# Routing inside the mix stage's block, ranks by products with ones, the last tile by halves, dummy products, the first slab in parts

## The chip, the cores and the metric

The kernel runs on one core of one Trainium2 chip. The metric is the device time of one launch in microseconds, here the median of three runs. The profiler adds one traced execution, from which the busy times and waits below come.

## The reference, cut to what matters

The program is two layers of a network on 512 tokens of width 1024, all in float32. The change lies in the first: behind its token mixer comes a feed-forward layer in which each of 16 experts chooses its 64 tokens.

```python
# y_lat: output of the token mixer before its norm (the mix stage computes it and all up to h)
x_lat = x_lat + gt1 * rmsnorm(y_lat, norm_post_mix)
h = rmsnorm(x_lat, norm_pre_ffn) * (1.0 + sc2) + sh2

def expert_choice_ffn(h, w_router, w_gate, w_up, w_down):
    cap = 2 * 512 // 16                                   # 64 tokens for each expert
    aff = softmax(h @ w_router, axis=-1)                  # [512, 16]
    top_aff, top_idx = lax.top_k(aff.T, cap)              # each expert's 64 best tokens
    xin = h[top_idx]                                      # [16, 64, 1024]
    g, u = xin @ w_gate, xin @ w_up                       # 16 experts, [1024, 1024] each
    y = ((silu(g) * u) @ w_down) * top_aff[..., None]
    return zeros(512, 1024).at[top_idx].add(y)
```

Order within an expert's 64 rows is free, since the rows are added back by index.

## The kernel before

The program is a sequence of stages, each in a block of its own; at a block's end all engines wait for each other. Inside a block every engine has a list of instructions written out by hand, and semaphores order them. The stages that matter here are `mix_and_project`, `route` and `experts`.

**`mix_and_project`** turns the mixer's rows (`turn_mix`, four tiles of 128 tokens), multiplies them by `w_out` (`product_hi`, `product_lo`, signalled half by half through `n.ready`), and takes each tile t through `norm_steps`: squares and root on ScalarE (`act_first`), gating and the addition to `x` on VectorE (`dve_gate`, `dve_add`, signalled by `n.added`), then the second norm's root (`act_root`) and eight transposes of `x` on TensorE (`turn`). ScalarE copies the first four turned blocks into `h2T` and VectorE the others (both called `take`). `logits(t)` multiplies them by the router's weights, `take_parts` copies the partial sums, `folded(t)` adds the four groups in a product and `take_logits` writes the tile's row of logits. The second norm's rows are also split into three bf16 parts (`act_full`, `dve_full`, `act_top`, `less`, `act_mid`, `low`), which the gather reads.

**`route`** makes the softmax over the 16 experts (VectorE, with one Exp on ScalarE), turns the affinities so that experts lie on 16 partitions, copies them to `left`, and finds each expert's 64 best tokens in eight rounds of a maximum of eight and a replacement by -1. `chosen` is then 1 where a value was replaced; a running sum over the tokens (`tensor_tensor_scan`) times `chosen` is the token's place, 1 to 64. Four transposes bring the places back to tokens on partitions (`posT`). While VectorE does this, TensorE runs 14 dummy products (`keep_busy`, a product of the identity into a bank that nobody reads). SyncE loads the first expert slab in five parts (`m.opening`: three of 512 KB, two of 256 KB) at the start of this stage.

**`experts`** streams 96 slabs of 2 MB (w_gate, w_up, w_down, two halves each, for 16 experts). Experts go in pairs. `mark(i)` on VectorE makes the one-hot matrix of a pair from `posT`. `gather(i)` on TensorE takes the pair's rows out of the three parts: 96 products into banks 0 and 1, then 4 with the identity (the transposed one-hot, `spread`) and 12 for the affinities. `take_in` copies the results: ScalarE blocks 0 to 3 of `xin`, then `spread` and the slot affinities; VectorE blocks 4 to 7. Then follow `up_product` for w_gate and w_up, the hidden rows' transposes and `down_product`. A slab has one of ten places. Slabs 0 to 9 are issued before the stage (0 in the opening places; 5, 4, 1, 2, 3 and 8 in the mix stage, 6, 7 and 9 in `route`). From slab 10 on, SyncE issues a slab when the one that held its place has been used: slab 10 waits for the second half of the first up product.

The order of the loads on SyncE's queue in `mix_and_project` before:

```python
sp.wait_ge(gated_out, TT);        stream(sp, m, I, S_EXP + 5, S_EXP + 6)
sp.wait_ge(n.ready, 2 * TT - 1);  stream(sp, m, I, S_EXP + 4, S_EXP + 5); stream(sp, m, I, S_EXP + 1, S_EXP + 2)
sp.wait_ge(n.ready, 2 * TT);      stream(sp, m, I, S_EXP + 2, S_EXP + 4)
stream(sp, m, I, S_EXP + 8, S_EXP + 9)
```

Of the kernel before, what the change touches and what calls it, by code (L numbers as in the profile page):

```python
# [1344 lines left out]
def norm_steps(m, tag, x, xn, st, gate=None, gated=None, weight=None, quarters=False):  # L1345
# [31 lines left out]
    def act_root(act, t):  # L1377
        act.wait_ge(n.added, t + 1)
# [23 lines left out]
    def dve_add(dve, t):  # L1402
# [7 lines left out]
        dve.wait_ge(n.gated, 2 * t + 2)  # L1410
        dve.scalar_tensor_tensor(out=x[:, t, :], in0=gated(t), scalar=st[:, 4, t:t + 1], in1=x[:, t, :],
# [13 lines left out]
    def turn(pe, t):  # L1425
# [115 lines left out]
def mix_and_project(nc, m, I):  # L1541
# [41 lines left out]
    lg = m.logits = m.rows_after[0][:, :].rearrange("p (t e) -> p t e", e=EXPERTS)  # L1583

# [12 lines left out]
    with nc.Block() as block:  # L1597
        @block.sync
        def _(sp):
# [4 lines left out]
            for r in range(2):  # L1604
                sp.dma_start(m.w_router[:, 4 * r:4 * r + 4, 0:EXPERTS],
                             I["w_router"][0].rearrange("(r p j) e -> r p j e", r=2, j=4)[r]).then_inc(m.router_in, 16)
            sp.wait_ge(gated_out, TT)
            stream(sp, m, I, S_EXP + 5, S_EXP + 6)
            sp.wait_ge(n.ready, 2 * TT - 1)
# [3 lines left out]
            stream(sp, m, I, S_EXP + 2, S_EXP + 4)  # L1613
            stream(sp, m, I, S_EXP + 8, S_EXP + 9)

        @block.gpsimd
        def _(pool):
            pool.memset(m.w_router[:, :, :], 0.0).then_inc(zeroed, 1)

        @block.tensor  # L1620
        def _(pe):
# [80 lines left out]
            for t in range(1, TT):  # L1702
# [11 lines left out]
                logits(t - 1)  # L1714
            folded(TT - 2)
            n.turn(pe, TT - 1)
            logits(TT - 1)
            folded(TT - 1)

        @block.scalar  # L1720
        def _(act):
# [51 lines left out]
            for t in range(TT):  # L1773
# [7 lines left out]
                if t:  # L1781
                    take_parts(t - 1)
                n.act_root(act, t)
# [3 lines left out]
            take(TT - 1)  # L1787
            take_parts(TT - 1)
            m.parts.act_full(act, TT - 1)

        @block.vector
        def _(dve):
# [100 lines left out]
            take_logits(TT - 1)  # L1893


def route(nc, m, I):
# [10 lines left out]
    chosen, place = [m.small(name, [E, T], at) for name, at in (("chosen", 0), ("place", 2 * KB))]  # L1907
    ones = m.ones[0:E, 0:1].to_broadcast([E, T])
    top = m.rows_after[2][0:E, 32:40]

    expd = m.sem("logit_exp_ready")
# [6 lines left out]
    place_ready = m.sem("place_ready")  # L1918
    place_turned = m.sem("place_turned")
    logit_less = m.sem("logit_less_max")  # L1920
    with nc.Block() as block:
        @block.sync
        def _(sp):
            first = slab_source(I, S_EXP)
            for k in range(3):
# [1942 lines left out]
```

## Time and profile before

| what | us |
| --- | --- |
| median of three runs (lowest, highest) | 1714.55 (1711.69, 1719.66) |
| profiled execution, its own time | 1718.3 |
| profiled execution, span of the trace | 1716.4 |
| TensorE busy (matmul) | 1622.8 |
| VectorE busy | 875.1 |
| ScalarE busy | 640.5 |
| GpSimd busy | 81.6 |
| granted TensorE clock, mean | 0.978 of full |

Times inside the trace count from the span's start. A busy TensorE is not TensorE at its peak: its matmuls overlap, and at the lower of its two clocks (1.2 and not 2.4 GHz, shown as 0.5) it is busy twice as long. A wait shows as the idle time of an engine, with the instruction that ended it. A transfer has an issue on SyncE's queue (`SPq`) and a time to landing, counted from the issue's start.

### The profile page before, as it was taken

How to read it: one execution, taken by the hardware profiler on the slowest of the kernel's cores; microseconds unless marked ns; L12 is line 12 of the kernel's file. 1: busy time of each engine (PE TensorE's matmuls, PEld its weight loads, DVE VectorE, ACT ScalarE, POOL GpSimd, SP SyncE). 2: the span in 40 equal slices, each digit the busy share in tenths (PEclk: the TensorE clock that was granted, in tenths of full speed). 3: DMA queues.
4: the chain of work that ended last, by engine and by line, in shares of the span. 5: the costliest groups of instructions: out<-in, count | busy, mean ns of one | idle time of the engine just before them, and what ended most of it. 6: DMA issues, size and time to landing. Idle time of an engine off the chain costs nothing. (4 is left out here: it accounts for less than half of the span.)

```text
span 1716.4 us, 26072 instructions
## 1 busy us (share of the span) xinstructions
PE 1622.8 (95%) x11074; PEld 1156.3 (67%) x11074; DVE 875.1 (51%) x1287; ACT 640.5 (37%) x1085; POOL 81.6 (5%) x69
## 2 busy tenths in 40 slices
PE   6999999988988999999999989998989999999997
PEld 4787888767764444334433378887878798888886
DVE  4445454189752122221221477754537638585768
ACT  4325774322551111011101244324465435454545
POOL 0010000000010000000000012211130000000000
PEclk9999999989989999999999989999999999999999
DMA  9221011246268999999999932210001270505111
GB/s 371 97 98 50 1 50 50 98 188 227 94 263 370 429 430 429 432 429 430 429 430 430 411 135 98 99 50 1 3 4 50 62 258 1 196 2 195 41 58 50
DMA packets 68764, 323.38 MB, mean 188 GB/s; under 512 B 6604, under 2 KB 11036, under 8 KB 55080
## 3 DMA queue, kind: packets, MB, share of 16 engines
q1 hardware_dynamic: 67768, 319.51, 46.7%
q8 instruction: 88, 1.44, 0.3%
q10 hardware_dynamic: 880, 2.20, 0.3%
q14 instruction: 28, 0.23, 0.0%
HBM read 315.41 MB, written 6.29 MB: 187 GB/s over the span
## 5 line engine op out<-in xcount | busy, mean ns | idle before, releaser
L3623 DVE TENSOR_TENSOR mlp_w_lo<-ring,mlp_w_hi 128x1024 fp32r<-128x1024 f32 x84 | 102.3, 1221 | 93.6 <-ACT mlp_w_hi L3558 93.4
L2190 PE MATMUL bank<-ring,xinT 128*64 128x512 f32 x528 | 117.8, 594 | 3.5 <-DMA ring<-w_gate 3.5
L2190 PE MATMUL bank<-expert_slab,xinT 128*64 128x512 f32 x480 | 107.2, 594 | 1.7 <-DMA expert_slab<-w_gate 1.7
L259 PE MATMUL bank<-h4T_hi,mlp_w_hi 128*128 128x512 f32 (+1 forms) x288 | 105.5, 366 | 0.3 <-PEq L3208 0.3
L259 PE MATMUL bank<-h4T_lo,mlp_w_hi 128*128 128x512 f32 (+1 forms) x288 | 105.2, 365 | 0.0
L259 PE MATMUL bank<-h4T_hi,mlp_w_lo 128*128 128x512 f32 (+1 forms) x288 | 105.2, 365 | 0.0
L3558 ACT ACTIVATE mlp_w_hi<-ring 128x1024 fp32r<-128x1024 f32 x84 | 88.8, 1057 | 38.6 <-PE bank L3512 38.6
L259 PE MATMUL bank<-hT_hi,in_w_hi 128*128 128x512 f32 (+1 forms) x256 | 96.9, 379 | 1.8 <-ACT v L630 1.8
L259 PE MATMUL bank<-hT_hi,in_w_lo 128*128 128x512 f32 (+1 forms) x256 | 90.0, 352 | 0.0
L259 PE MATMUL bank<-hT_lo,in_w_hi 128*128 128x512 f32 (+1 forms) x256 | 89.7, 350 | 0.0
L2190 PEld LDWEIGHTS bank<-ring,xinT 128*64 128x64 f32 x528 | 37.8, 137 | 75.6 <-issue 71.7
L3512 PE MATMUL bank<-mlp_w_hi,mlp_rows_hi 128*128 128x512 f32 x224 | 87.4, 390 | 1.4 <-DVE x L3679 1.4
L603 DVE TENSOR_TENSOR in_w_lo<-ring,in_w_hi 128x1024 fp32r<-128x1024 f32 x31 | 42.4, 1368 | 87.9 <-ACT in_w_hi L597 87.9
L3512 PE MATMUL bank<-mlp_w_hi,mlp_rows_lo 128*128 128x512 f32 x224 | 87.2, 389 | 0.0
L3512 PE MATMUL bank<-mlp_w_lo,mlp_rows_hi 128*128 128x512 f32 x224 | 87.1, 389 | 0.0
L2190 PEld LDWEIGHTS bank<-expert_slab,xinT 128*64 128x64 f32 x480 | 34.4, 137 | 67.3 <-issue 65.2
L2292 ACT ACTIVATE expert_out_hi<-bank 64x512 fp32r<-64x512 f32 x32 | 18.9, 591 | 146.8 <-PE bank L2210 146.3
L2351 DVE TENSOR_TENSOR expert_out_lo<-bank,expert_out_hi 64x512 fp32r<-64x512 f32 x32 | 22.0, 689 | 100.3 <-ACT expert_out_hi L2292 99.8
L2338 DVE SCALAR_TENSOR_TENSOR expert_hidden<-bank,slot_affinity,gate_sig 128x512 f32<-128x512 f32 x16 | 18.0, 1124 | 99.9 <-PE bank L2190 56.4
L2210 PE MATMUL bank<-expert_slab,expert_hiddenT 128*64 128x512 f32 x288 | 66.1, 607 | 2.4 <-DMA expert_slab<-w_down 2.4
L597 ACT ACTIVATE in_w_hi<-ring 128x1024 fp32r<-128x1024 f32 x31 | 32.7, 1056 | 90.0 <-PE bank L259 87.7
L259 PE MATMUL bank<-h3T_hi,gdn_w_hi 128*128 128x512 f32 x160 | 62.4, 390 | 0.0
(520 smaller groups left out, 3633.3 us busy)
## 6 DMA issues: line engine op xcount, KB each, us to landing
expert_slab<-w_down SPq DMA_DIRECT2D x18, 2048.0 KB, 28.1
ring<-w_up SPq DMA_DIRECT2D x17, 2048.0 KB, 22.6
ring<-w_gate SPq DMA_DIRECT2D x16, 2048.0 KB, 21.3
expert_slab<-w_gate SPq DMA_DIRECT2D x15, 2048.0 KB, 22.8
expert_slab<-w_up SPq DMA_DIRECT2D x15, 2048.0 KB, 24.2
ring<-mlp_w SPq DMA_DIRECT2D x15, 2048.0 KB, 8.5
ring<-w_down SPq DMA_DIRECT2D x14, 2048.0 KB, 25.3
ring<-w_ada SPq DMA_DIRECT2D x8, 2048.0 KB, 7.8
```

The source lines that it names most:

```text
L259: mm = pe.matmul(out, x, y, start=(start and i == 0), stop=(stop and i == 2))
L597: act.activation(shaped_buffer(q)[0], slab_part(m, s, i, by_rows), ACT.Copy).then_inc(m.in_w_hi_ready, 1)
L603: dve.tensor_tensor(lo, slab_part(m, s, i, by_rows), hi, ALU.subtract).then_inc(m.in_w_lo_ready, 1)
L2190: mm = pe.matmul(bank[half * H:(half + 1) * H, b, :], xin[:, 4 * r + k, (e % 2) * H:(e % 2 + 1) * H], expert_part(m, s, k, half), start=(r ...
L2210: mm = pe.matmul(bank[half * H:(half + 1) * H, 7, :], hidT[:, k, r * H:(r + 1) * H], expert_part(m, s, k, half), start=(r == 0 and k == 0) ...
L2292: act.activation(m.y[0][r * H:(r + 1) * H, half * COLS:(half + 1) * COLS], bank[half * H:(half + 1) * H, 7, :], ACT.Copy).then_inc(y_hi, 1)
L2338: dve.scalar_tensor_tensor(out=hid[:, :].rearrange("p (j q) -> p q j", j=4), in0=bank[:, b + 1, :].rearrange("p (q j) -> p q j", j=4), sca ...
L2351: dve.tensor_tensor(m.y[1][dst], bank[half * H:(half + 1) * H, 7, :], m.y[0][dst], ALU.subtract).then_inc(y_lo, 1)
L3512: mm = pe.matmul(bank[:, 4 + 2 * pair + t, :], a[:, k, tok], b[:, k, :], start=(anew and i % 2 == 0 and k == 0 and n == 0), stop=(i % 2 == ...
L3558: act.activation(buffer_of(unit)[0], weight_source(unit), ACT.Copy).then_inc(w_hi, 1)
L3623: dve.tensor_tensor(lo, weight_source(unit), hi, ALU.subtract).then_inc(w_lo, 1)
```

## The change

- **Last tile by halves.** In tile 3 `dve_add` adds `x` in two instructions of 512 columns; `turn` starts its first four transposes behind the first, ScalarE's `take(3)` comes ahead of `act_root(3)`.
- **Routing in the mix stage's block.** `route` has no block of its own. It gives each engine a list that is appended to that of `mix_and_project`; VectorE's begins with a wait for the last logits. ScalarE begins with an Exp on a value that nobody reads; `act_full(3)` comes behind the real Exp.
- **Ranks by products.** The first maximum and replacement read the turned affinities from their bank, with no copy. What is left after the rounds is turned back to tokens on partitions and compared with 0 there (`chosen`, [128, 64]). One product with `m.upto` (ones where row <= column) and three with ones, accumulated, give the running sum over tokens; one multiplication gives `posT`.
- **Dummy products.** `keep_busy` takes a number of columns. There is one of 512 and two of 256 columns in the tail of the mix stage, two of 512 ahead of the affinities' transposes, 13 (before 14) behind them, and one of 256 ahead of the first gather.
- **First slab in parts.** Parts 0, 1 and 3 are issued behind the last `turn_mix`, part 2 behind the third tile's `low`, part 4 behind the last logits and `act_full(3)`; slab 8 now comes after part 4.
- **Gather.** In every `gather` the 4 and 12 short products come first. `gathered` is signalled twice, for blocks 0 to 3 and 4 to 7; ScalarE copies `spread` and the affinities first. The wait for VectorE's blocks (`xin_v`) moves to the second slab of the w_gate product.

```diff
-def keep_busy(pe, m, b, n):
+def keep_busy(pe, m, b, n, cols=COLS):
...
-        pe.matmul(m.bank[:, b, :], m.ident, m.table[:, 0:COLS], start=True, stop=True)
+        pe.matmul(m.bank[:, b, 0:cols], m.ident, m.table[:, 0:cols], start=True, stop=True)
...
     def act_root(act, t):
-        act.wait_ge(n.added, t + 1)
+        act.wait_ge(n.added, t + 2 if quarters and t == TT - 1 else t + 1)
...
+        if quarters and t == TT - 1:
+            for i in range(2):
+                dve.scalar_tensor_tensor(out=x[:, t, cols(i)], in0=gated(t)[:, cols(i)], scalar=st[:, 4, t:t + 1], in1=x[:, t, cols(i)],
+                                         op0=ALU.mult, op1=ALU.add).then_inc(n.added, 1)
+            return
...
         for k in range(KD):
+            if quarters and t == TT - 1 and k == 4:
+                pe.wait_ge(n.added, TT + 1)
...
             sp.wait_ge(gated_out, TT)
             stream(sp, m, I, S_EXP + 5, S_EXP + 6)
+            sp.wait_ge(mix_turned, 2 * TT)
+            for i in (0, 1, 3):
+                opening(i)
             sp.wait_ge(n.ready, 2 * TT - 1)
             stream(sp, m, I, S_EXP + 4, S_EXP + 5)
             stream(sp, m, I, S_EXP + 1, S_EXP + 2)
             sp.wait_ge(n.ready, 2 * TT)
             stream(sp, m, I, S_EXP + 2, S_EXP + 4)
+            sp.wait_ge(m.parts.low_done, TT - 1)
+            opening(2)
+            sp.wait_ge(logits_out, TT)
+            sp.wait_ge(m.parts.full, 2 * TT)
+            opening(4)
             stream(sp, m, I, S_EXP + 8, S_EXP + 9)
+            stream(sp, m, I, S_EXP + 6, S_EXP + 7)
+            sp.wait_ge(m.x_kept, 16 * TT)
+            stream(sp, m, I, S_EXP + 7, S_EXP + 8)
+            stream(sp, m, I, S_EXP + 9, S_EXP + 10)
...
+            keep_busy(pe, m, 5, 1)
             folded(TT - 2)
+            keep_busy(pe, m, 5, 1, COLS // 2)
             n.turn(pe, TT - 1)
+            keep_busy(pe, m, 5, 1, COLS // 2)
             logits(TT - 1)
             folded(TT - 1)
+            choice.tensor(pe)
...
+                if t == TT - 1:
+                    take(t)
                 n.act_root(act, t)
...
-            take(TT - 1)
             take_parts(TT - 1)
-            m.parts.act_full(act, TT - 1)
+            choice.scalar(act)
...
+    def tensor(pe):
+        keep_busy(pe, m, 5, 2)
+        pe.wait_ge(aff_ready, 1)
+        for t in range(TT):
+            mm = pe.transpose(bank[0:E, 1, t * P:(t + 1) * P], aff[:, t, :], m.ident)
+        mm.then_inc(aff_turned, 1)
+        keep_busy(pe, m, 5, CAP // 8 + 5)
+        pe.wait_ge(ranked, 1)
+        for t in range(TT):
+            mm = pe.transpose(bank[:, 2, t * E:(t + 1) * E], left[:, t * P:(t + 1) * P], m.ident[0:E, 0:E])
+        mm.then_inc(ranked_turned, 1)
+        pe.wait_ge(chosen_ready, 1)
+        pe.matmul(bank[:, 3, 0:TT * E], m.upto, chosen, start=True, stop=False)
+        for t in range(1, TT):
+            mm = pe.matmul(bank[:, 3, t * E:TT * E], m.ones[:, :], chosen[:, 0:(TT - t) * E], start=False, stop=(t == TT - 1))
+        mm.then_inc(place_ready, 1)
+
+    def scalar(act):
+        act.activation(unused, m.eps[:, :], ACT.Exp)
+        act.wait_ge(logit_less, 1)
+        act.activation(ex[:, :, :], lg[:, :, :], ACT.Exp).then_inc(expd, 1)
+        parts.act_full(act, TT - 1)
...
-            link(dve.tensor_copy(left[:, :], bank[0:E, 1, :]))
-
-            for _ in range(CAP // 8):
-                link(dve.max(top[:, :], left[:, :]))
-                link(dve.match_replace(left[:, :], top[:, :], left[:, :], -1.0))
-            link(dve.tensor_scalar(chosen[:, :], left[:, :], 0.0, None, ALU.is_lt))
-
-            link(dve.tensor_tensor_scan(place[:, :], ones, chosen[:, :], 0.0, ALU.mult, ALU.add))
-            dve.tensor_tensor(place[:, :], place[:, :], chosen[:, :], ALU.mult).then_inc(place_ready, 1)
-            dve.wait_ge(place_turned, 1)
-            dve.tensor_copy(m.posT[:, :, :], bank[:, 2, 0:TT * E].rearrange("p (t e) -> p t e", e=E))
...
+        for i in range(rounds):
+            now = left[:, :] if i else bank[0:E, 1, :]
+            link(dve.max(top[:, :], now))
+            taken = dve.match_replace(left[:, :], top[:, :], now, -1.0)
+            if i + 1 < rounds:
+                link(taken)
+        taken.then_inc(ranked, 1)
+        dve.wait_ge(ranked_turned, 1)
+        dve.tensor_scalar(chosen, bank[:, 2, 0:TT * E], 0.0, None, ALU.is_lt).then_inc(chosen_ready, 1)
+        dve.wait_ge(chosen_ready, 1)
+        dve.wait_ge(place_ready, 1)
+        dve.tensor_tensor(m.posT[:, :, :], bank[:, 3, 0:TT * E].rearrange("p (t e) -> p t e", e=E),
+                          chosen.rearrange("p (t e) -> p t e", e=E), ALU.mult)
...
+                    if k % 4 == 3:
+                        mm.then_inc(gathered, 1)
...
+                    if r and e % 2 == 0 and name == "g":
+                        pe.wait_ge(xin_v, e // 2 + 1)
...
+            keep_busy(pe, m, 5, 1, COLS // 2)
             gather(0)
```

## Rows read from the trace of the kernel before

**Rows 1.** The page, forty slices of the span (tenths of the transfer engines' time)

```profile
DMA  9221011246268999999999932210001270505111
```

**Rows 2.** Windows: us, busy time of each engine, granted clock, DMA share, GB/s

```profile
475.00:489.00 14.00, 14.00 (x86) 11.47 (x85) 8.35 (x14) 8.16 (x15) 0.00 (x0) 1.00 0.10 39
...
538.00:542.00 4.00, 4.00 (x20) 1.55 (x18) 0.00 (x0) 0.12 (x1) 0.00 (x0) 1.00 0.05 20
...
546.00:760.00 214.00, 211.95 (x1308) 90.13 (x1306) 48.36 (x75) 27.83 (x66) 0.00 (x0) 1.00 1.01 430
760.00:965.00 205.00, 193.88 (x1114) 79.61 (x1108) 49.23 (x76) 26.17 (x59) 0.00 (x0) 0.99 1.01 429
```

**Rows 3.** Waits in 760 to 972 us: total, times, longest

```profile
PE bank L2190 <- DMA ring<-w_gate: 3.5, 3, 1.3
```

**Rows 4.** Timeline of SyncE's queue: start and length of issue, us

```profile
510.82 0.82 SPq L229 DMA_DIRECT2D expert_slab<-w_down  x1
...
541.88 3.76 SPq L229 DMA_DIRECT2D ring<-w_gate  x2
```

**Rows 5.** Transfers issued in 511 to 512 and 541 to 542.5 us: to landing

```profile
expert_slab<-w_down SPq DMA_DIRECT2D x1, 2048.0 KB, 27.7
...
ring<-w_gate SPq DMA_DIRECT2D x1, 2048.0 KB, 8.1
```

**Rows 6.** Timeline of the last tile's end, all engines: start, length in us

```profile
497.37 1.28 DVE L1411 SCALAR_TENSOR_TENSOR x<-out_gated,out_stats,x 128x1024 f32<-128x1024 f32 x1
...
498.69 1.06 ACT L1379 ACTIVATE xn<-x 128x1024 f32<-128x1024 f32 x1 [1.53 <-DVE x L1411]
...
498.71 1.61 PE L1435 MATMUL bank<-table,x 128*128 128x128 f32 x8 [1.11 <-DVE x L1411]
...
501.20 1.08 PE L1661 MATMUL bank<-h2T,w_router 128*32 128x128 f32 x16 [0.88 <-DVE h2T L1806]
...
503.31 0.23 DVE L1824 SCALAR_TENSOR_TENSOR router_rows<-bank,out_stats,router_bias 128x16 f32<-128x16 f32 x1 [1.38 <-PE bank L1673]
```

**Rows 7.** Timeline of earlier tiles, TensorE

```profile
476.02 1.19 PE L1435 MATMUL bank<-table,x 128*128 128x128 f32 x8
...
482.65 0.64 PE L1661 MATMUL bank<-h2T,w_router 128*32 128x128 f32 x16
```

**Rows 8.** Timeline of the routing stage, all engines

```profile
503.94 1.28 ACT L1949 ACT_TABLE_LOAD   x1 [0.27 <-PEq L1597]
503.97 0.22 DVE L1970 TENSOR_REDUCE router_rows<-router_rows 128x4 f32<-128x64 f32 x1 [0.43 <-PEq L1597]
...
505.23 0.26 ACT L1949 ACTIVATE router_rows<-router_rows 128x64 f32<-128x64 f32 x1
...
506.26 1.02 PE L1938 MATMUL bank<-table,affinity 128*16 128x128 f32 x4 [2.99 <-DVE affinity L1975]
...
507.08 13.42 PE L266 MATMUL bank<-table 128*128 128x512 f32 x28
507.33 0.68 DVE L1977 COPY aff_left<-bank 16x512 f32<-16x512 f32 x1 [1.12 <-PE bank L1938]
...
508.04 0.68 DVE L1980 MAX8 router_rows<-aff_left 16x8 f32<-16x512 f32 x1
...
519.98 0.42 DVE L1982 TENSOR_SCALAR chosen<-aff_left 16x512 f32<-16x512 f32 x1
...
522.86 0.22 DVE L1987 COPY placeT<-bank 128x64 f32<-128x64 f32 x1 [0.51 <-PE bank L1943]
```

**Rows 9.** Timeline of the first gather and the next one

```profile
524.13 0.61 PE L2172 MATMUL bank<-onehot,xn_top 128*128 128x128 bf16 x4 [1.31 <-DVE onehot L2301]
...
534.76 3.65 PE L2190 MATMUL bank<-opening,xinT 128*64 128x512 f32 x16 [1.78 <-ACT spread L2266]
...
563.12 0.40 PE L2172 MATMUL bank<-onehot,xn_top 128*128 128x128 bf16 x4
...
569.09 3.65 PE L2210 MATMUL bank<-ring,expert_hiddenT 128*64 128x512 f32 x16
```

More of the change, by code:

```diff
@@ L1906, in route @@
     left = m.arena("aff_left", [E, T], 90)
-    chosen, place = [m.small(name, [E, T], at) for name, at in (("chosen", 0), ("place", 2 * KB))]
-    ones = m.ones[0:E, 0:1].to_broadcast([E, T])
+    chosen = m.rows_after[0][:, :]
     top = m.rows_after[2][0:E, 32:40]
+    r = Shared()
     expd = m.sem("logit_exp_ready")
@@ new lines, in scalar @@
+    def scalar(act):
[3 more added lines that the diff above has]
+        parts.act_full(act, TT - 1)
+        parts.act_top(act, TT - 1)
+        act.activation(m.ident_narrow[:, :], m.ident, ACT.Copy)
+        act.wait_ge(aff_ready, 1)
+        act.activation(m.aff_parts[:, 0], aff[:, :, :], ACT.Copy).then_inc(aff_top, 1)
+        parts.act_mid(act, TT - 1)
+        act.wait_ge(aff_less, 1)
+        act.activation(m.aff_parts[:, 1], less[:, :, :], ACT.Copy).then_inc(aff_mid, 1)
@@ L1990, in output_norms @@
+    r.tensor, r.scalar, r.gpsimd, r.vector = tensor, scalar, gpsimd, vector
+    return r
 def output_norms(m, done):
@@ L2168, in gather @@
                     pe.wait_ge(summed, NS * (i - 1))
-                for k in range(KD):
-                    for part in range(3):
-                        for t in range(TT):
-                            mm = pe.matmul(bank[:, k // 4, (k % 4) * P:(k % 4 + 1) * P], xn2_part(m, part, t, k), m.onehot[:, t, :],
-                                           start=(part == 0 and t == 0), stop=(part == 2 and t == TT - 1))
-                mm.then_inc(gathered, 1)
                 for t in range(TT):
@@ L2181, in gather @@
                                        start=(part == 0 and t == 0), stop=(part == 2 and t == TT - 1))
-                mm.then_inc(onehot_used, 1)
+                mm.then_inc(spread_turned, 1)
+                for k in range(KD):
+                    for part in range(3):
+                        for t in range(TT):
+                            mm = pe.matmul(bank[:, k // 4, (k % 4) * P:(k % 4 + 1) * P], xn2_part(m, part, t, k), m.onehot[:, t, :],
+                                           start=(part == 0 and t == 0), stop=(part == 2 and t == TT - 1))
+                    if k % 4 == 3:
+                        mm.then_inc(gathered, 1)
             def up_product(e, name, b, part_ready, ready):
@@ L2257, in take_in @@
             def take_in(i):
-                act.wait_ge(gathered, i + 1)
-                for k in range(4):
-                    ins = act.activation(xin[:, k, :], bank[:, 0, k * P:(k + 1) * P], ACT.Identity,
-                                         scale=m.a2[:, k:k + 1], bias=m.mod[:, 16 + k, 0:1])
-                ins.then_inc(xin_a, 1)
-                act.wait_ge(onehot_used, i + 1)
+                act.wait_ge(spread_turned, i + 1)
                 if i >= 2:
@@ L2270, in take_in @@
                                        bank[r * H:(r + 1) * H, 3, r:r + 1], ACT.Copy).then_inc(slot_aff_ready, 1)
+                act.wait_ge(gathered, 2 * i + 1)
+                for k in range(4):
+                    ins = act.activation(xin[:, k, :], bank[:, 0, k * P:(k + 1) * P], ACT.Identity,
+                                         scale=m.a2[:, k:k + 1], bias=m.mod[:, 16 + k, 0:1])
+                ins.then_inc(xin_a, 1)
             take_in(0)
```

93 lines of the change are left out of this document (33 added, 60 removed).

## The prediction, made before the changed kernel was timed

> **What bounds the kernel now.** I read the page first, then windows over the stretch that the change touches, then who waits, then the transfers one by one, then the timeline. In the page's forty slices the DMA row is full from the fourteenth slice to the twenty-third [rows 1]: that is the expert stage, which streams 96 slabs of 2 MB. The windows sharpen it [rows 2]: from 546 to 965 us the transfer engines are at 1.01 and move 429 to 430 GB/s. TensorE is idle for 2.05 of 214 us up to 760, and for 11.1 of 205 us after it; among the longest waits of that second part is one for slabs [rows 3], and up to 760 the same view has no wait for a slab at all. So TensorE starts with ten slabs in memory, catches up with the transfers at 760, and from there runs at their pace: the end of the stage is the arrival of the last slab. Everything behind it hangs on that, so a microsecond of the stage's end is one of the span.
>
> When does the last slab land? The transfers run without a hole except one: in 538 to 542 the share is 0.05 [rows 2]. All slots are full there, and the queue waits for TensorE to release the first. The tenth slab of the preload was issued at 510.82 and took 27.7 us, so it landed at 538.5; the next was issued at 541.88 and took 8.1, landing at 549.98 [rows 4, 5]. At 429 GB/s a slab (2.097 MB) takes 4.89 us. The hole thus costs 549.98 - 538.5 - 4.89 = 6.6 us. After it the queue is never empty, so the rest of the stage is a rigid train behind that one issue.
>
> That gives the account. Gain = how much earlier that slab lands, and two things limit it: **A**, how much earlier TensorE gets there (the slot is released two slabs into its first up product); **B**, what the transfers can do: 6.6 us of hole, plus what is moved ahead of the full stretch. In 475 to 489 us the share is 0.10 [rows 2], so parts 0, 1 and 3 of the first slab (512 + 512 + 256 KB = 1.31 MB), now issued behind the last turn of the mix rows, at about 476, are free there and take 1.31/0.429 = 3.1 us from the full stretch. B = 9.7 us.
>
> **The change part by part, for A.**
>
> *Last tile by halves.* Before, x is added in one instruction at 497.37 to 498.65, the eight transposes take 1.61 us, the logits start at 501.20 and the last row of logits is out at 503.54 [rows 6]. After: the first 512 columns are ready at about 498.06 (half of 1.28 and 0.05 of overhead), four transposes 0.6 (eight take 1.19 at the full clock [rows 7]) run while the second half is added (to 498.75); the other four end at 499.4 and not 500.3, and the logits, which wait for VectorE's copy of them, start at about 500.2: 1.0 earlier. At full clock they take 0.64 and not 1.08 [rows 6, 7]: 0.4 more. ScalarE now copies its half (an estimate from the square's 1.06 for twice the columns: 0.6) ahead of the square and the root, so these end 0.6 later, at about 500.85, just as the logits end: no loss, but no slack. Saved: 1.4 (bounds: 0.9 without the clock, 1.6).
>
> *Routing inside the block.* Between 503.54 and 505.23 lie the block's end (0.43), two VectorE steps of 0.22 and a table load of 1.28 that only starts at 503.94 [rows 8]. Now a throwaway Exp is put right behind ScalarE's copy of the logit parts (about 501.2), so the load is over at 502.5 and the throwaway at 502.75; the logits are at 502.1, the maximum taken off at 502.65. Exp starts at about 502.75 and not 505.23: saved 2.5 in all, 1.1 of it here. The row of Exp starts 0.01 after the load ends. The Trainium skill (ScalarE: Activation LUTs, What ACT_TABLE_LOAD costs) puts a drain of 1.38 behind each load; by it, as an estimate, Exp would start at 504.1, and the sum would be 8.4 and not 9.7.
>
> *Transposes of the affinities, and no copy.* Four transposes of 1.02 at the lower clock become about 0.6 if the clock holds: 0.4. VectorE's copy of 0.68 goes, since the first maximum reads the bank [rows 8]; I take a maximum from a bank at the copy's price from a bank, which is that of the maximum (0.68 both). With the gap, 0.7. Sum so far 3.6. The eight rounds (508.04 to 519.98, 11.9 us) stay.
>
> *Ranks by products.* From 519.98 to 523.08, 3.1 us: comparison, scan, product on 16 partitions, four transposes, copy [rows 8]. After: four transposes (at most 0.5, by the copy's wait), a comparison on 64 columns (0.22 like the copy), four products, one multiplication (0.22). No row has these products; 16 of 128 columns take 0.64 [rows 7], and four with 64 columns or fewer can hardly take less than 0.3; I take 0.6. With four hand-overs of 0.05: 1.7. Saved 1.4 (1.1 to 1.7). Sum 5.0.
>
> *Gather.* Its first matmul is at 524.13, and the up product starts at 534.76, 10.6 us later; the next pair's gather takes 569.09 - 563.12 = 5.97 [rows 9]. Of the difference 1.8 is the wait on ScalarE's `spread` (the row of 534.76), which the new order inside `gather` takes away: the one-hot products come first, so `spread` and the first four blocks of `xin` are copied under the rest, and VectorE's four blocks are only asked for by the second slab, 3.4 us later. The other 2.9 is the clock: the first 96 products ran mostly at 1.2 GHz (0.61 for four [rows 9], 0.39 later). If the new dummies (one of 256 columns ahead of the gather) and the shorter gaps hold the clock, both are saved: 4.7; if not, 1.8. Sum A = 9.7, or 6.8.
>
> *What costs nothing.* The other dummies: one ahead of each short piece of the tail, two ahead of the affinity transposes, 13 behind them. Fourteen took 13.42 [rows 8]; less 1.2 for a start of about 2.4 us at the lower clock, one takes 0.87 at full speed and 1.74 at half (estimates). Two from 501.65 end at 503.4, the affinities come at 503.7; 13 from 504.35 end at 515.65, the last round at 516.3. They are covered by 0.3 and 0.65 us, which is thin (see rivals). Later gathers: same work in another order, with a down product of 7 us behind each. SyncE: slab 8 is now queued behind part 4, which waits for the last logits and for `act_full` behind Exp (about 504.2, where before it was issued with slabs 2 and 3), and slabs 6, 7 and 9 after it. The transfers issued by then (four slabs from 489, part 2) last until about 511, so 6 us of cover; each microsecond beyond is one of loss. One barrier less for all engines is in the 2.5 above.
>
> **The sum.** A = 9.7 and B = 9.7 agree, so I forecast 9.6. Against its own execution: 1716.4 - 9.6 = 1706.8 span, with the 1.9 around it 1708.7. That execution is 3.75 above the median; on the median, 1714.55 - 9.6 = 1705.0.
>
> **Rivals.**
> 1. *The clock falls ahead of the gather.* TensorE has some 1.5 us of work in the 3.6 between the 13th dummy and the gather. It fell in the tail of before after short pieces and gaps (0.5 from 500 us by the doubled logits, rows 6). Then A = 6.8: 1714.55 - 6.8 = 1707.8.
> 2. *The dummies become the chain.* If the clock already falls in the tail, logits and fold cost 0.6 more, two dummies at 1.2 GHz take 2 x 1.74 = 3.5 and hold the affinity transposes until 505.8, these take 1.02, the first maximum is at 506.9 (saved 1.1, not 3.6), the 13 dummies end at 519.4 and the rounds at 518.8 (0.6 more lost). A = 1.1 - 0.6 + 1.4 + 1.8, with 2.9 if the clock is back: 3.7 to 6.6, so 1708 to 1711. The Trainium skill (TensorE: Matmul & The Clock Gate, Part 4: PE-mode transpose) says that transposes don't count as busy for the clock; by it the tail, half of which is transposes, points to this rival; in rows 6 the clock falls around transposes, but behind gaps too, so they don't decide it.
> 3. *Slower: the 13 dummies at 1.2 GHz.* At 1.74 each they are 22.6 us. For every microsecond that the clock stays low in them the ranks are 0.5 later; from 5.0 us saved (rival 2 with the low clock in the gather too: 519.98 - 506.9 - 11.3 = 1.8, and 1.4, and 1.8) the change is at zero after 10 us at the low clock, and at 22.6 it is 6.3 slower: 1720.9. Against it: before, some 2.4 us of the same dummies were low.
> 4. *The hole stays.* If slots are released no earlier in effect, or the queue behind part 4 runs dry as much as is won, only the 3.1 us of moved parts are left: 1711.5. Against it: the 6 us of cover.
> 5. *A drain behind the throwaway load*, as the skill's rule in the part on routing: 8.4, so 1706.2. Mechanism: ScalarE idle behind its load. The Exp row speaks against it.
>
> **Chances.** The forecast 0.52 (its own range 1704 to 1706.5), rival 1 0.22, rival 2 0.08, rival 3 0.04, rival 4 0.06, rival 5 0.03, and 0.05 for more than B (gaps elsewhere in the span that shift). A measurement tells 0.5% (8.6 us, so 1706.0) from no change. The forecast lies 1 us beyond that and the runs shown scatter by 2.9 below and 5.1 above their median, so 0.8 of its chance counts as faster: 0.42, with the last case 0.47 faster. Slower is rival 3 and 0.02 for scatter, 0.06; the rest, 0.47, is within. Range: from 1705.0 less the lower scatter, 1702, to the end of rivals 2 and 4, 1711.5.
>
> **What the changed profile would show.** Parts 0, 1, 3 issued near 476; no window under a share of 0.9 between 491 and 960; the first reuse of a slot issued near 532.2 and landing near 540.3; Exp with its load ended before; first up product near 525 with no wait; four gather products of 0.39 from the first on and the granted clock at 1.00 from 497 to 530. TensorE's waits for slabs after 750 as before. A clock of 0.5 around 502 or 520 is rival 2 or 1; a dummy ending right at the affinity transposes or the last transposes is rival 2 or 3. I am wrong if the last slab's landing moves by less than the first reuse does.

## The result, and the profile after

The changed kernel takes 1702.5 us (median of four runs, 1702.2 to 1706.3), the kernel before 1713.4 on the same chip (1711.7 to 1719.7). The ratio is 0.9938, with a 95% interval from 0.9919 to 0.9956, which is 7.5 to 13.9 us. The forecast was 1705.0.

The profiled execution has a span of 1700.4 us against 1716.4, but 6.6 of these 16.0 are no part of the change: slab 4 is issued at 482.50 and was at 489.09, and every instruction ahead of it that TensorE's path depends on is the same in both. What differs is the granted clock, the third number from the end in the windows up to that issue, before and after:

```profile
0.00:489.09 489.09, 455.86 (x3363) 364.88 (x3363) 267.66 (x412) 219.63 (x368) 15.26 (x20) 0.97 0.33 118
0.00:482.50 482.50, 450.89 (x3363) 360.99 (x3364) 267.24 (x412) 219.77 (x368) 15.59 (x20) 0.99 0.34 123
```

It goes with the execution and not with the kernel: a second trace of the changed kernel (x_again, below) has the issue at 482.9, and its variants have it at 483.3 to 488.2, the last of them at a clock of 0.97. So all distances in this part are counted **from the issue of slab 4**. By that count the end of the span comes at 1217.9 and was at 1227.3: 9.4 earlier.

The windows of the changed kernel, with the columns of [rows 2]:

```profile
475.00:489.00 14.00, 14.00 (x79) 11.07 (x78) 7.89 (x12) 7.08 (x13) 0.00 (x0) 1.00 0.49 187
489.00:534.00 45.00, 42.06 (x273) 22.59 (x274) 20.48 (x48) 13.28 (x30) 4.92 (x5) 0.96 0.99 412
534.00:546.00 12.00, 12.00 (x60) 4.11 (x58) 1.81 (x2) 1.18 (x2) 0.00 (x0) 1.00 1.00 429
546.00:760.00 214.00, 211.28 (x1298) 89.82 (x1296) 52.83 (x83) 28.95 (x67) 0.00 (x0) 1.00 1.01 430
760.00:965.00 205.00, 191.40 (x1100) 78.80 (x1100) 47.49 (x72) 30.63 (x65) 0.00 (x0) 0.99 1.01 428
```

The hole of 538 to 542 us, at 20 GB/s, is no longer there, but a dip is left in its place that these long windows hide. Around the issue of slab 10 (the first that reuses a slot) the transfers move 235 GB/s for 3 us and not 430:

```profile
527.50:530.50 3.00, 3.00 (x16) 1.00 (x14) 0.69 (x1) 0.60 (x1) 0.00 (x0) 1.00 0.76 235
```

In the last stretch TensorE still idles for 13.6 of 205 us, and it waits for slabs as in [rows 3]:

```profile
PE bank L2226 <- DMA ring<-w_gate: 3.6, 3, 1.3
...
PE bank L2226 <- DMA expert_slab<-w_gate: 2.4, 2, 1.3
```

So the stage's end is still the arrival of the last slab. SyncE's queue (start and length of issue), with below it the time to landing of the transfers issued in 527.5 to 528.3 us:

```profile
469.26 1.29 SPq L1619 DMA_DIRECT2D opening<-w_gate  x3
482.50 0.33 SPq L229 DMA_DIRECT2D expert_slab<-w_gate  x1
...
490.03 7.96 SPq L1619 DMA_DIRECT2D opening<-w_gate  x2
498.04 0.44 SPq L229 DMA_DIRECT2D ring<-w_down  x1
...
505.09 0.43 SPq L229 DMA_DIRECT2D expert_slab<-w_down  x1
...
527.83 0.33 SPq L229 DMA_DIRECT2D ring<-w_gate  x1
```

```profile
ring<-w_gate SPq DMA_DIRECT2D x1, 2048.0 KB, 8.1
```

Slab 10 is issued at 527.83, a distance of 45.33 where it was 52.79 [rows 4]: **7.46 us earlier**, and it takes the same 8.1 to land [rows 5]. The timeline between, with the columns of [rows 6]:

```profile
490.77 1.42 DVE L1413 SCALAR_TENSOR_TENSOR x<-out_gated,out_stats,x 128x512 f32<-128x512 f32 x2
...
493.87 0.65 PE L1688 MATMUL bank<-h2T,w_router 128*32 128x128 f32 x16 [0.44 <-DVE h2T L1838]
...
494.86 1.28 ACT L1974 ACT_TABLE_LOAD   x1
...
495.33 0.23 DVE L1856 SCALAR_TENSOR_TENSOR router_rows<-bank,out_stats,router_bias 128x16 f32<-128x16 f32 x1
...
496.16 0.20 ACT L1974 ACTIVATE router_rows<-eps 128x1 f32<-128x1 f32 x1
496.27 0.24 ACT L1976 ACTIVATE router_rows<-router_rows 128x64 f32<-128x64 f32 x1
...
497.29 0.60 PE L1960 MATMUL bank<-table,affinity 128*16 128x128 f32 x4 [0.18 <-DVE affinity L2002]
...
497.73 11.32 PE L266 MATMUL bank<-table 128*128 128x512 f32 x26
497.93 0.69 DVE L2007 MAX8 router_rows<-bank 16x8 f32<-16x512 f32 x1 [0.70 <-PE bank L1960]
...
509.18 0.66 DVE L2008 MATCH_REPLACE8 aff_left<-router_rows,aff_left 16x512 f32<-16x512 f32 x1
509.90 0.42 PE L1965 MATMUL bank<-table,aff_left 16*128 16x16 f32 x4 [0.85 <-DVE aff_left L2008]
510.36 0.23 DVE L2013 TENSOR_SCALAR router_rows<-bank 128x64 f32<-128x64 f32 x1 [0.51 <-PE bank L1965]
510.63 0.43 PE L1968 MATMUL bank<-router_rows,table 128*128 128x64 f32 x2 [0.32 <-DVE router_rows L2013]
510.91 0.79 PE L1970 MATMUL bank<-router_rows,ones 128*128 128x48 f32 x6
511.81 0.23 DVE L2016 TENSOR_TENSOR placeT<-bank,router_rows 128x64 f32<-128x64 f32 x1 [1.23 <-PE bank L1970]
...
513.09 0.40 PE L2203 MATMUL bank<-ident_narrow,onehot 128*128 128x128 bf16 x4
...
514.10 0.63 PE L2213 MATMUL bank<-onehot,xn_low 128*128 128x128 bf16 x4
...
520.70 3.65 PE L2226 MATMUL bank<-opening,xinT 128*64 128x512 f32 x16
```

Three things are to be seen. The table load is over before Exp is due, and the throwaway follows it in 0.02 us. The four products of the running sum (with `m.upto` and with ones, the rows of L1968 and L1970) take 1.07 us from 510.63, the longest piece of the ranks. And the gather starts with four products in 0.40 us, but from 514.10 four take 0.63: TensorE has fallen to the lower of its two levels (1.2 GHz, not 2.4) in the midst of products that follow each other without a gap. The granted clock of the windows shows both, the full clock in the tail and the fall:

```profile
489.00:497.50 8.50, 7.44 (x57) 4.03 (x57) 5.29 (x15) 5.98 (x13) 0.00 (x0) 1.00 1.01 425
497.50:510.00 12.50, 11.65 (x32) 5.05 (x29) 11.39 (x24) 2.78 (x7) 4.92 (x5) 1.00 1.00 419
510.00:521.00 11.00, 9.97 (x128) 9.20 (x130) 1.33 (x4) 3.93 (x10) 0.00 (x0) 0.84 1.01 432
```

### The profile page after: what moved, and what is told of

Same layout as the page of the kernel before. It is cut to its first block and busy times, and to the rows that moved or that the text cites. A ratio compares the mean times of both kernels' runs of the same rounds, so it can differ in the third digit from the quotient of the medians.

```text
span 1700.4 us, 26105 instructions
## 1 busy us (share of the span) xinstructions
PE 1616.7 (95%) x11092; PEld 1148.4 (68%) x11092; DVE 872.1 (51%) x1285; ACT 641.8 (38%) x1086; POOL 82.0 (5%) x69
## 3 DMA queue, kind: packets, MB, share of 16 engines
q1 hardware_dynamic: 67768, 319.51, 47.2%
## 5 line engine op out<-in xcount | busy, mean ns | idle before, releaser
L2374 DVE SCALAR_TENSOR_TENSOR expert_hidden<-bank,slot_affinity,gate_sig 128x512 f32<-128x512 f32 x16 | 18.0, 1124 | 99.9 <-PE bank L2226 56.4
L3619 ACT ACTIVATE mlp_relu<-bank 128x512 f32<-128x512 f32 x32 | 19.1, 598 | 115.8 <-PE bank L259 115.8
```

The costliest lines, as they stand in the source:

```text
L2374: dve.scalar_tensor_tensor(out=hid[:, :].rearrange("p (j q) -> p q j", j=4), in0=bank[:, b + 1, :].rearrange("p (q j) -> p q j", j=4), sca ...
L3619: act.activation(r[:, u % 2, :], bank[:, u % 4, :], ACT.Relu).then_inc(relu, 1)
```

## The experiments

Every kernel is told by the same chain: the gather starts, the first up product starts, slab 10 is issued, the slab before it lands, slab 10 lands, the last slab lands. In us from the issue of slab 4, worked out of each trace's rows; landings are issue plus time to landing. Each row is one trace. The ratio is to the kernel before, from four runs of the changed kernel and six to twelve of each other one; the kernel before had medians of 1713.4, 1714.5, 1714.4 and 1712.5 in the four sessions.

| kernel | gather | it lasts | up product | slab 10 issued | slab 9 lands | slab 10 lands | last lands | ratio |
| --- | --- | --- | --- | --- | --- | --- | --- | --- |
| before | 35.0 | 10.6 | 45.7 | 52.8 | 49.4 | 60.9 | 479.2 | 1 |
| x_parts_alone | 35.0 | 10.6 | 45.7 | 52.8 | 46.7 | 60.6 | 478.7 | 0.9993 |
| x_delay_first | 37.5 | 6.0 | 43.5 | 50.6 | 46.2 | 58.7 | 477.0 | 0.9992 |
| x_delay_second | 30.6 | 7.6 | 38.2 | 45.3 | 46.9 | 54.6 | 474.1 | 0.9966 |
| x_parts_late | 30.6 | 7.5 | 38.1 | 45.2 | 49.6 | 55.7 | 473.4 | 0.9972 |
| x_both_late | 30.6 | 6.8 | 37.4 | 44.5 | 50.2 | 56.4 | 473.1 | 0.9974 |
| x_delay_small | 30.6 | 6.0 | 36.6 | 43.7 | 46.2 | 53.8 | 472.1 | 0.9964 |
| x_scan | 31.5 | 7.4 | 39.0 | 46.1 | 46.7 | 54.2 | 471.7 | 0.9963 |
| x_no_dummies | 33.1 | 6.0 | 39.1 | 46.2 | 46.6 | 54.7 | 471.6 | 0.9966 |
| x_gather_old | 30.6 | 8.4 | 39.0 | 46.1 | 47.1 | 54.2 | 471.5 | 0.9958 |
| changed | 30.6 | 7.6 | 38.2 | 45.3 | 46.9 | 53.4 | 471.0 | 0.9938 |
| x_again | 30.6 | 7.6 | 38.2 | 45.3 | 47.2 | 53.8 | 470.8 | 0.9934 |
| x_delay_late | 30.6 | 7.5 | 38.1 | 45.2 | 46.6 | 53.8 | 470.4 | 0.9952 |
| x_warm | 30.8 | 6.0 | 36.8 | 43.9 | 46.4 | 52.5 | 469.7 | 0.9946 |

**x_again.** The changed kernel, unedited.

> The changed kernel once more. Theory (the stage's end follows the first reuse of a slot, which came 7.5 us earlier in the trace): 7.5 to 9.5 us under the kernel before, a ratio of 0.9945 to 0.9956. Rival (more is won than the expert stage shows, for the medians differ by 10.9): 10 us or more, 0.994 or less.

Measured: 1704.7 us, ratio 0.9934 (0.9915 to 0.9952). Its chain is that of the changed kernel to 0.4 us. The ratio is the rival's (11.3 us) and not the theory's; the interval reaches into the theory's band, but slab 10 lands only 7.1 earlier than before, and that is outside it.

**x_no_dummies.** The new dummies left out; the 13 behind the affinities' transposes stay.

```diff
-            keep_busy(pe, m, 5, 1)
             folded(TT - 2)
-            keep_busy(pe, m, 5, 1, COLS // 2)
             n.turn(pe, TT - 1)
-            keep_busy(pe, m, 5, 1, COLS // 2)
...
-        keep_busy(pe, m, 5, 2)
         pe.wait_ge(aff_ready, 1)
...
-            keep_busy(pe, m, 5, 1, COLS // 2)
             gather(0)
```

> The changed kernel without the new dummy products in the tail, ahead of the affinity transposes and ahead of the first gather; the 13 stay. Theory (they hold TensorE's clock through the tail): logits, fold and transposes at 1.2 GHz again, 1.2 us later, and the gather low to about 3 us instead of 1.6: the first reuse 1.5 to 3 us later and the span as much longer than the changed kernel's. Rival (the clock does not hang on them, and they only fill): the same within 0.5 us. Second rival (they sit in the chain): up to 1 us shorter.

Measured: 1709.5 us, ratio 0.9966 (0.9951 to 0.9980). The windows of its tail and of its rounds, and TensorE's timeline:

```profile
493.00:500.00 7.00, 3.88 (x31) 2.82 (x32) 3.63 (x11) 5.49 (x10) 0.00 (x0) 0.63 0.99 403
500.00:514.00 14.00, 14.00 (x31) 5.84 (x30) 11.39 (x24) 2.19 (x6) 4.92 (x5) 0.82 1.02 425
```

```profile
499.18 1.02 PE L1956 MATMUL bank<-table,affinity 128*16 128x128 f32 x4 [1.86 <-DVE affinity L1998]
499.99 13.86 PE L266 MATMUL bank<-table 128*128 128x512 f32 x26
513.79 0.42 PE L1961 MATMUL bank<-table,aff_left 16*128 16x16 f32 x4
```

The clock falls in the tail, the 13 dummies take 13.9 us and not 11.3, and the last round's replacement had ended at 512.1: the dummies hold the transposes for 1.7 us. The gather starts 2.5 later. But then it runs at the full clock throughout, which gives 1.6 back; what is left is 0.9 at the issue and 0.6 at the last landing, less than the 1.5 to 3 that I expected. That is the mechanism of my rival 2, on the kernel without the new dummies. The ratio is further off the changed kernel's (2.8 thousandths, 4.8 us) than the 0.6 us of the last landing would explain. The trace is not a typical one: two of the twelve runs, the traced one among them, take 1702.6 and 1703.6 at a mean granted clock of 0.986, the other ten 1708.0 to 1711.6 at 0.979 to 0.983 (x_again: 0.986 to 0.990). Where in those ten the clock is lower no trace shows.

**x_delay_first.** Six dummies ahead of the first gather.

```diff
             keep_busy(pe, m, 5, 1, COLS // 2)
+            pe.wait_ge(onehot_ready, 1)
+            keep_busy(pe, m, 5, 6)
             gather(0)
```

> The changed kernel with six dummy products of 512 columns (5.2 us) between the one-hot matrix and the first gather. They also bring the clock up, so the gather should take 6.0 and not 7.6 us: a net delay of 3.5 us of the first reuse of a slot. Theory (rigid train): the last slab lands 3.5 us later and the span is 3.5 us longer than the changed kernel's. Rival (TensorE has over 10 us of waits for slabs behind 760, so a delay at the start is absorbed): the same span within 0.7 us, and 3.5 us less of those waits.

Measured: 1713.1 us, ratio 0.9992 (0.9974 to 1.0009). The gather starts 6.9 later and takes 1.6 less; the remaining 5.3, where I expected 3.5, stand in the issue of slab 10, in its landing (5.3), and in the last landing (6.0). The train behind slab 10 is rigid but for 0.7 us, and the whole gain of the change can be taken away at this one place.

**x_delay_second.** Four dummies ahead of the second gather.

```diff
+                if e == 1:
+                    pe.wait_ge(onehot_ready, 2)
+                    pe.wait_ge(hid_ready, 1)
+                    keep_busy(pe, m, 2, 4)
                 if e % 2 and e < EXPERTS - 1:
```

> The changed kernel with four dummy products of 512 columns (3.4 us) ahead of the gather of the second pair, where the transfer queue has slabs outstanding. Theory: the next slot is released 3.4 us later, but its slab was 11.8 us from issue to landing where 8.1 is what an empty queue needs, so 3.7 us are covered and nothing moves: the same span as the changed kernel's within 0.7 us, TensorE's waits for slabs 3.4 us less. Rival (any work on TensorE in this stage lengthens it): 3.4 us longer.

Measured: 1709.7 us, ratio 0.9966 (0.9951 to 0.9982): missed. Slab 10 is issued at the same distance, but the last slab lands 3.1 later. 1.2 of it is slab 10's own (it lands 9.3 behind its issue), which the edit can't have caused, and 2.8 comes at slabs 17 and 18 (some of the sum is given back in other steps). These are issued 4.0 and 3.6 ahead of the landing of the slab before, in the changed kernel 6.9 and 4.9, and land 6.5 and 6.1 behind that landing, in the changed kernel 4.9 both. A queue that isn't empty is thus no full cover.

**x_warm.** Three more short dummies between the transposes, the products with ones and the mark.

```diff
         keep_busy(pe, m, 5, CAP // 8 + 5)
+        keep_busy(pe, m, 5, 1, COLS // 2)
...
         mm.then_inc(ranked_turned, 1)
+        keep_busy(pe, m, 5, 1, P)
...
         mm.then_inc(place_ready, 1)
+        keep_busy(pe, m, 5, 1, COLS // 2)
```

> The changed kernel with three more dummy products where TensorE still idles between the rounds' end and the gather: one of 256 columns behind the 13, one of 128 behind the transposes of the ranks, one of 256 behind the products with ones. Theory (rival 1 of the prediction: gaps ahead of the gather let the clock fall in it): the clock stays at full rate through the gather, which takes 6.0 and not 7.6 us; the first reuse of a slot comes 43.7 us behind the issue of slab 4 and not 45.3, and the last landing and the end 1.6 us earlier than in the changed kernel. Rival (the clock falls there whatever the gaps): no gain, and up to 0.2 us lost behind the dummies.

Measured: 1705.0 us, ratio 0.9946 (0.9931 to 0.9962). Rows of its gather:

```profile
517.52 0.40 PE L2206 MATMUL bank<-ident_narrow,onehot 128*128 128x128 bf16 x4
...
518.50 0.39 PE L2216 MATMUL bank<-onehot,xn_low 128*128 128x128 bf16 x4
```

It takes 5.99 us to the up product, the 5.97 of [rows 9]: the full clock is worth 1.6. Slab 10 is issued at 43.9, as expected, but lands only 0.9 earlier than in the changed kernel. Two other kernels with no such dummies kept the clock: x_delay_small, which is the changed one up to the gather, and x_both_late, which holds loads back and has the old order inside the gather; so this one execution does not show that the dummies did it. And x_warm isn't measurably faster than the changed kernel.

**x_gather_old.** The gather's old order of products and copies; its two signals for the halves stay.

```diff
             def take_in(i):
+                act.wait_ge(gathered, 2 * i + 1)
+                for k in range(4):
+                    ins = act.activation(xin[:, k, :], bank[:, 0, k * P:(k + 1) * P], ACT.Identity,
...
                 act.wait_ge(spread_turned, i + 1)
...
-                    dve.wait_ge(gathered, 2 * i)
+                    dve.wait_ge(spread_turned, i)
...
```

> The changed kernel with the order inside every gather as before: the 96 products first, then the one-hot and affinity products; ScalarE copies its blocks of xin first and then spread. Theory (TensorE waits for spread ahead of the first up product): the wait of 1.8 us is back, the first reuse of a slot at 47.1 us behind the issue of slab 4 and not 45.3, the end 1.8 us later than the changed kernel's. Rival (the order is hidden): no difference.

Measured: 1707.3 us, ratio 0.9958 (0.9943 to 0.9973). The gather lasts 0.8 longer, not 1.8. Its up product in the timeline:

```profile
525.22 3.65 PE L2226 MATMUL bank<-opening,xinT 128*64 128x512 f32 x16 [0.73 <-issue]
```

In [rows 9] this idle time was 1.78. The rest of it may lie with the copies of blocks 0 to 3, which start behind half of the products in this kernel too and in the kernel before only behind all of them; no run separates that.

**x_scan.** Comparison, scan and product on 16 partitions, as before, in place of the products with ones.

```diff
+        link(dve.tensor_scalar(taken_from[:, :], left[:, :], 0.0, None, ALU.is_lt))
+        link(dve.tensor_tensor_scan(place[:, :], ones, taken_from[:, :], 0.0, ALU.mult, ALU.add))
+        dve.tensor_tensor(place[:, :], place[:, :], taken_from[:, :], ALU.mult).then_inc(place_ready, 1)
...
```

> The changed kernel with the ranks as before: comparison, scan and multiplication on 16 partitions, four transposes, a copy. Theory: from the last replacement to the places 3.1 us and not 2.2, so 0.9 us later, and as TensorE is idle for longer ahead of the gather up to 1.2 us more for a gather at the lower clock: the first reuse at 46.2 to 47.4 us behind the issue of slab 4. Rival (the products with ones cost as much as the scan): 45.3, no difference.

Measured: 1707.7 us, ratio 0.9963 (0.9949 to 0.9977). The gather starts 0.95 later, slab 10 is issued 0.8 and the last slab lands 0.7 later. So the products with ones are worth 0.9 and not 1.4.

**x_parts_late.** All five parts of the first slab behind the last logits.

```diff
-            sp.wait_ge(mix_turned, 2 * TT)
-            for i in (0, 1, 3):
-                opening(i)
...
-            sp.wait_ge(m.parts.low_done, TT - 1)
-            opening(2)
+            stream(sp, m, I, S_EXP + 8, S_EXP + 9)
...
-            opening(4)
-            stream(sp, m, I, S_EXP + 8, S_EXP + 9)
+            for i in range(5):
+                opening(i)
```

> The changed kernel with all five parts of the first slab issued behind the last logits, and slab 8 ahead of them. Theory (the slots' first reuse is issued at 45.3 us whatever the parts do, and its slab lands one step of 4.9 us behind the preload, whose end moves from 47 to 50 us): that slab lands at 55.0 and not 53.6, so the end is 1.5 us later than the changed kernel's. Rival 1 (the parts are worth their full transfer time): 3.1 us later. Rival 2 (hidden): no difference.

Measured: 1710.6 us, ratio 0.9972 (0.9958 to 0.9986). TensorE is as early as in the changed kernel, but slab 10 takes longer to land:

```profile
ring<-w_gate SPq DMA_DIRECT2D x1, 2048.0 KB, 10.6
```

It lands 2.3 later, and so does the last slab (2.4): between my 1.5 and the 3.1 of rival 1, since slab 9 lands 2.7 later and the step behind it is 6.1 and not 4.9. With the parts late the transfers are the limit.

**x_parts_alone.** The kernel before, with parts 0, 1 and 3 issued behind the last turn of the mix rows.

```diff
+            sp.wait_ge(mix_turned, 2 * TT)
+            for i in (0, 1, 3):
+                src = first[:, i, :] if i < 3 else first[:, 3, 0:COLS]
+                sp.dma_start(m.opening[i][:, :], src).then_inc(m.slab_loaded[OPENING], 16)
             sp.wait_ge(n.ready, 2 * TT - 1)
...
```

> The kernel before, with one edit: parts 0, 1 and 3 of the first slab are issued behind the last turn of the mix rows; part 2 and part 4 stay in the routing. Distances are from the issue of slab 4. In the kernel before, the preload has landed at 49.40, the first reuse of a slot is issued at 52.79 and lands 8.10 later, at 60.89. Theory (the reused slab lands 8.1 us behind its issue when the queue is empty, whatever was moved ahead): the preload ends at about 46.3, the issue stays at 52.8, the landing at 60.9, and the time does not change: within 0.999 and 1.001. Rival (as my fourth rival had it: the 3.1 us of moved transfers are a gain by themselves): landing at 57.8, ratio 0.998.

Measured: 1713.1 us against 1712.5, ratio 0.9993 (0.9977 to 1.0010). The preload ends 2.7 earlier, the hole is longer by as much, and slab 10 lands 0.3 earlier. The parts are worth nothing alone and 2.3 with TensorE early.

**x_both_late.** Late parts and the gather's old order together.

> The changed kernel with both the parts of the first slab late (all five in the place of before, behind the last logits) and the old order inside the gather. The late parts alone gave the landing of the reused slab at 55.74 from the issue of slab 4, 6.14 behind the slab before it; the old order alone moved it from 53.44 to 54.15. Theory (the landing is the later of issue + 8.1 and the landing before + 6.13): with the issue at about 45.9 the second one decides, the landing stays at 55.7, and the old order costs nothing here. Rival (the two losses add up): 56.4.

Measured: 1708.6 us, ratio 0.9974 (0.9957 to 0.9991). The clock held in this gather, so slab 10 is issued 0.7 earlier than in x_parts_late; it lands 11.9 behind its issue and 6.2 behind slab 9, whose own landing is 0.6 later. The figure of 56.4 was the rival's, but it doesn't come about by a sum: the issue moved the other way. What holds is the step behind slab 9, 6.1 to 6.2 in x_warm, x_parts_late and here, with the issue 2.5, 4.4 and 5.7 ahead of that landing; x_delay_small, with 2.5, took 7.7.

**x_delay_small.** One dummy where x_delay_second has four.

> The changed kernel with one dummy of 512 columns (0.88 us at 2.4 GHz by the run with four) ahead of the second pair's gather. In the changed kernel slab 18 is issued 4.94 us ahead of the landing of slab 17 and lands 4.89 behind it; with four dummies it was issued 3.57 ahead and landed 6.14 behind. Theory (a slab that is issued less than some 4.5 us ahead of the landing before it costs 1.25 us, once, whatever is missing): slab 18 issued 4.06 ahead, a step of 6.14, and all later slabs 1.25 later than in the changed kernel: more than the delay that causes it. Rivals: the queue covers it, as it is never empty: 0; or the delay passes through as it is: 0.9.

Measured: 1705.4 us, ratio 0.9964 (0.9951 to 0.9978). It decides nothing: slab 18 was issued 6.9 ahead of the landing before it and not 4.1, and landed 4.9 behind it. The clock held in its first gather, so slab 18 was issued 0.7 earlier than in the changed kernel, and slab 17 landed 1.3 later, after two long steps (7.7 at slab 10, 6.4 at slab 13). The threshold that I expected stays untested. And a held clock didn't pay at the landing here: slab 10, issued 1.6 earlier than in the changed kernel, landed 0.4 later.

**x_delay_late.** The same four dummies at the sixth gather.

```diff
+                if e == 9:
+                    pe.wait_ge(onehot_ready, 6)
+                    pe.wait_ge(hid_ready, 9)
+                    keep_busy(pe, m, 2, 4)
```

> The changed kernel with four dummies of 512 columns (3.5 us) ahead of the sixth pair's gather, at expert 9, where slabs are issued over 12 us ahead of the landing before them. Theory (a delay is paid for only where the queue is about to run dry): no landing moves, the last slab lands at 471 from the issue of slab 4 and the time is that of the changed kernel, ratio 0.993 to 0.996. Rival (TensorE is the bound in the expert stage, and every delay in it counts): 3.5 us at the end of the span, as the same 3.5 to 5.3 us counted ahead of the first gather.

Measured: 1703.7 us, ratio 0.9952 (0.9936 to 0.9968). TensorE's timeline, and its wait for slabs in 560 to 980 us:

```profile
770.98 3.70 PE L266 MATMUL bank<-table 128*128 128x512 f32 x8
774.52 0.39 PE L2203 MATMUL bank<-ident_narrow,onehot 128*128 128x128 bf16 x4
```

```profile
PE bank L2226 <- DMA ring<-w_gate: 2.0, 2, 1.1
```

That wait was 3.6 in the changed kernel; all of TensorE's waits for slabs together fall from 8.7 to 5.5. The 3.5 us of dummies come out of them, and the last slab lands at 470.4. A delay that costs up to its whole length ahead of the first gather costs nothing here.

## Why the prediction was right, and which terms were off

**What sets the end: confirmed.** The first reuse of a slot does, and the stage behind it is a train. x_delay_first moves it and the end together, x_delay_late moves neither, and down the table the ratio follows the last landing, with scatter, from 0.9993 to about 0.994.

**Tail, Exp, transposes, no copy: 3.6 foretold, 3.5 measured.** The first maximum is at 15.43 from slab 4's issue and was at 18.95 [rows 8]. Each step of it stands within 0.3 of the prediction; the shares of the single edits are read from this one trace, and no run takes them apart. Rival 5 falls (its sum should have been 8.3 and not 8.4, and the 1.38 in it is shown by no row): the throwaway starts 0.02 behind the load. The Trainium skill (ScalarE: Activation LUTs, What ACT_TABLE_LOAD costs) has a drain of 1.38 there; the trace does not agree.

**Ranks: 1.4 foretold, 0.9 measured.** The term that was mis-sized is the four products of the running sum: 0.6 taken, 1.07 measured; the whole is 2.2 us (509.84 to 512.04) and not 1.7. I had taken them near the lower bound. Sum to the gather 4.45, not 5.0.

**Gather: 4.7 foretold, 3.0 measured.** The step that failed is "the shorter gaps hold the clock". They held it in the gather's first microsecond only, and the fall took 1.6 of the 2.9. This is a part of rival 1, and it isn't settled by the code: with the same TensorE instructions up to there the gather lasts 7.5 to 7.6 us in five traces (changed, x_again, x_delay_second, x_delay_late, x_parts_late) and 6.0 in x_delay_small's.

So A = 7.46 and not 9.7: 0.55 is lost in the ranks and 1.6 in the clock.

**B: 9.7 foretold, 7.9 to 8.4 by what the traces show.** The preload ends 2.5 earlier and not 3.1 (46.9 where it was 49.4), and I had let slab 10 follow it at 4.89. It never did, the shortest step in the table is 6.1: it needs about 8.0 from its issue or 6.1 behind slab 9, whichever is later, and some executions add to that, up to 1.5 (x_delay_small). In the changed kernel's trace this is the dip to 235 GB/s: a window under a share of 0.9, which I had ruled out. With slab 9's landing at 46.4 to 46.9, B is 60.9 - 6.1 - 46.4 = 8.4, or 7.9. x_warm has A = 8.9 and gains 8.4 at the landing, x_delay_small has A = 9.1 and gains 7.1. So even with the clock held, 9.7 was out of reach.

**The sum was luckier than its terms.** The landing of slab 10 gives 7.5. The last landing is 8.2 earlier and the end of the span 9.4. The two additions come from unchanged work: from the last landing to the end the fourteen traces take between 745.1 and 748.2, and from slab 10's landing to the last one 416.6 to 418.3 in all but x_delay_second. The ratio says 10.6 us, with 7.5 just inside its interval (and outside that of x_again); the four kernels whose last slab lands earliest (changed, x_again, x_delay_late, x_warm) average 0.9943, or 9.8. So the chain's 7.5 to 8.4 explains most of the gain and not all. The rest may be clock in unchanged stages: the stretch ahead of slab 4 alone differs by up to 6.6 us between traces, and the mean granted clock was 0.984 to 0.988 in the changed kernel's four runs and 0.977 to 0.985 in 29 runs of the kernel before (the session of x_again). Whether that is chance or comes of the change stays open.

**The dummies: not the chain, as forecast, and worth having** (0.6 us by the trace without them, 4.8 by the times, most of that unexplained). In the changed kernel the 13 dummies end 0.85 ahead of the last transposes. Rival 2's mechanism appeared when the new ones were left out. The granted clock is 1.00 over 489 to 510 us with eight transposes in the tail, where without the dummies it is 0.63 over 493 to 500; gaps and transposes can't be told apart by that, so the rule of the Trainium skill (TensorE: Matmul & The Clock Gate, Part 4: PE-mode transpose) that transposes don't count as busy stays neither shown nor refuted. **Rivals 3 and 4** did not come: the clock stayed up in the dummies, and the queue behind part 4 did not run dry.

## What to carry to other kernels

In a stage that is bound by transfers, look for the one transfer that waited for compute, and count every edit by how much earlier it lands: what is behind it is a train, what is ahead of it pays in full only up to the second limit. Two edits that lift two limits of the same transfer must be priced together; one of them alone was worth nothing here, and undoing it later cost 2.3 us. And count distances in a trace from the last instruction that both kernels share, since whole executions drift by several microseconds before they reach it, here with the granted clock.

## What the runs showed of the hardware

- A 2 MB slab behind an empty queue lands 7.8 to 8.1 us after its issue (x_parts_alone, x_delay_first, before); in the kernel before the transfers moved 208 GB/s in its first 3 us, against 430 later. Issued 0.4 to 1.9 us ahead of the landing before it, it takes 8.05 to 9.3. In a full train a slab lands 4.9 behind the one before.
- In between there is a step of 6.1 to 6.2, for slab 10 in three kernels and for slab 18 in x_delay_second, though the queue held another slab for 2.5 to 5.7 us (6.5 at slab 17 there, 7.7 at slab 10 in x_delay_small). Its cause wasn't found, and the lead alone doesn't decide it: slab 18 issued 4.9 ahead and slab 11 issued 4.7 ahead in the changed kernel had no such step, slab 10 issued 5.7 ahead in x_both_late had.
- Single steps in the train are longer: 6.14, 6.17 and 6.16 in the kernel before, at slabs 16, 50 and 87; 5.4 to 5.5 in the changed kernel, at slabs 42, 48, 78 and 82. They come with 11 to 31 us of transfers in the queue.
- The same instructions find TensorE's clock at either level: in the first gather it fell in five executions and not in a sixth. A forecast that needs the level in one short stretch has a coin in it, here of 1.6 us.
- The gather ran at the full clock throughout in x_no_dummies, with an idle 1.38 us right ahead of it, after a stretch at 0.82 in the dummies.
